# Scattering the gates of an expert lookup: a kernel whose one-hot matrices move from two engines to one

## The reference, cut to what matters

```python
def _peer(x, wq, k1, k2, u_tab, v_tab):
    ...
    sc, pos = lax.top_k(cand, PEER_TOPK)                      # 16 of the candidates, for each of 8 heads
    eidx = jnp.take_along_axis(cidx, pos, axis=-1).reshape(T, PEER_HK)     # 128 experts of 16384 a token
    gate = jax.nn.softmax(sc.astype(jnp.float32), axis=-1).astype(x.dtype).reshape(T, PEER_HK)
    ...
        act = jax.nn.gelu(jnp.einsum('td,tkd->tk', xb, ub), approximate=False)
        vb = jnp.take(v_tab, ib, axis=0)
        return jnp.einsum('tk,tkd->td', gb * act, vb)
```

## Time and profile before

| | |
|---|---|
| three executions | 3152.38, 3154.97, 3155.89 us; median 3154.97 |
| the profiled execution, first to last instruction | 3147.6 us |
| median less that span | 7.4 us |
| PE busy | 2982.5 us, 95% |
| DVE busy | 2251.5 us, 72% |
| ACT busy | 1839.0 us, 58% |
| POOL busy | 1117.7 us, 36% |
| mean granted TensorE clock | 0.974 of full speed |
| gelu of pair 17 to gelu of pair 57, first lookup | 1483.00 to 1767.08 us |
| the same, second lookup | 2468.20 to 2752.02 us |

### The profile page before, as it was taken

One profiled execution on the slowest core, in us unless ns is written; L12 is line 12 of the kernel. 1 busy time (PEld: TensorE's weight loads), 2 busy tenths in 40 slices (PEclk: granted clock), 3 DMA queues, 4 the chain that ended last, 5 costly groups with the idle time before them and its releaser, 6 DMA issues.

```text
span 3147.6 us, 48399 instructions
## 1 busy us (share of the span) xinstructions
PE 2982.5 (95%) x17718; PEld 2613.9 (83%) x17718; DVE 2251.5 (72%) x3884; ACT 1839.0 (58%) x2813; POOL 1117.7 (36%) x1033
## 2 busy tenths in 40 slices
PE   7889999897999979898999999998989999999998
PEld 7768888776888857798999988887789999988887
DVE  5459999345899976598565487776579765557777
ACT  4658888444788855455555555555554555555554
POOL 3420000432000005688767501014569767620100
PEclk9989999998999989999999999999999999999999
DMA  5359999532899953465665677775346655677776
GB/s 205 114 189 350 374 370 370 182 141 86 303 374 369 365 187 118 134 188 192 191 185 181 211 248 238 245 239 183 128 135 213 186 189 180 186 237 245 240 243 205
DMA packets 203995, 701.76 MB, mean 223 GB/s; under 512 B 23602, under 2 KB 24754, under 8 KB 203504
## 3 DMA queue, kind: packets, MB, share of 16 engines
q1 hardware_dynamic: 170640, 619.07, 58.1%
q10 hardware_dynamic: 21056, 40.07, 3.5%
q0 software_dynamic: 12064, 39.52, 3.2%
HBM read 659.77 MB, written 38.80 MB: 222 GB/s over the span
## 4 chain that ended last, share of the span: by engine, by line
PE 87%; DVE 6%; POOL 3%; ACT 2%; DMA 1%; issue 1%; ACTq 0%; DVEq 0%; SPq 0%; POOLq 0%
PE ps L592 85%; POOL splitb L533 3%; PE ps L603 2%; DVE hrow L105 1%; DVE arena L95 1%; DVE arena L105 1%; ACT splitb L506 1%; DMA rawb<-in_peer_u 1%; DVE arena L100 0%; DVE hL L95 0%; DMA hrow<-in_x_rows 0%; ACT hH L159 0%; DMA spill<-gb 0%; ACT arena L159 0%; DMA rawb<-in_s_out 0%
## 5 line engine op out<-in xcount | busy, mean ns | idle before, releaser
L506 ACT ACTIVATE splitb<-rawb 128x512 fp32r<-128x512 f32 (+1 forms) x1306 | 826.7, 639 | 851.8 <-PE ps L592 708.4
L533 POOL TENSOR_TENSOR splitb<-rawb,splitb 128x512 fp32r<-128x512 f32 x571 | 775.3, 1374 | 855.9 <-ACT splitb L506 848.7
L592 PE MATMUL ps<-hH,splitb 128*128 128x256 f32 x5248 | 987.8, 287 | 18.8 <-POOL splitb L533 16.4
L592 PEld LDWEIGHTS ps<-hH,splitb 128*128 128x128 f32 x5248 | 836.9, 194 | 26.1 <-issue 14.3
L533 DVE TENSOR_TENSOR splitb<-rawb,splitb 128x512 fp32r<-128x512 f32 (+1 forms) x735 | 524.7, 733 | 409.1 <-ACT splitb L506 407.0
L592 PE MATMUL ps<-splitb,hid 128*128 128x512 f32 x3444 | 788.8, 389 | 2.6 <-ACT hid L159 2.6
L592 PEld LDWEIGHTS ps<-splitb,hid 128*128 128x128 f32 x3444 | 646.1, 188 | 138.4 <-ACT hid L159 3.4
L592 PE MATMUL ps<-hL,splitb 128*128 128x256 f32 x2624 | 747.2, 285 | 0.0
L592 PEld LDWEIGHTS ps<-hL,splitb 128*128 128x128 f32 x2624 | 508.4, 194 | 0.9 <-issue 0.5
L592 PE MATMUL ps<-experts_r 128*128 128x512 f32 (+2 forms) x1364 | 338.3, 397 | 16.5 <-ACT experts_r L159 9.0
L592 PEld LDWEIGHTS ps<-experts_r 128*128 128x128 f32 (+1 forms) x1364 | 256.6, 194 | 72.5 <-ACT experts_r L159 7.5
(11 more groups left out here) (163 smaller groups left out, 3320.2 us busy)
## 6 DMA issues: line engine op xcount, KB each, us to landing
rawb<-in_peer_u SPq DMA_DIRECT2D x256, 512.0 KB, 3.7
rawb<-in_peer_v SPq DMA_DIRECT2D x256, 512.0 KB, 4.2
experts<-in_moe_gu SPq DMA_DIRECT2D x228, 512.0 KB, 5.5
experts<-in_moe_d SPq DMA_DIRECT2D x108, 512.0 KB, 5.3
rawb<-in_moe_gu SPq DMA_DIRECT2D x92, 512.0 KB, 5.5
spill<-gb ACTq DMA_DIRECT2D x128, 256.0 KB, 4.2
aux<-spill POOLq DMA_DIRECT2D x128, 256.0 KB, 4.4
rawb<-in_moe_d SPq DMA_DIRECT2D x52, 512.0 KB, 5.5
```

The lines of the kernel that those rows point to most:

```text
L506: self.eng.activation(S.split(m)[0], S.raw(n)[:, off:off + w], ACT.Copy).then_inc(S.hi.sem, S.hi.step(("half", m)))
L533: self.eng.tensor_tensor(l, raw, h.bitcast(F32), ALU.subtract).then_inc(self.low.sem, self.low.step(("half", m), *([("raw", n)] if last el ...
L592: return self.eng.matmul(o, w, x, start=start, stop=stop)
```

## The change

For a token there is now one fp32r matmul of 128 x 256 in place of an fp32 one of 128 x 128. Its moving operand holds the i1 one-hot twice, times the high part and times the low part of the gate (`low` is gate minus its fp32r rounding; `dve_low_gates` makes it once for all tokens). The high and the low page stand beside each other in PSUM: for two tokens (a `k`), one bank. ScalarE copies the low page to `Gt` (`act_high_sum`), VectorE then adds the high page from PSUM (`dve_sum`). VectorE makes all one-hots: for two tokens one TENSOR_TENSOR of 128 x 256 and two SCALAR_TENSOR_TENSORs of 128 x 256. GpSimd makes no one-hots and all low halves up to pair 57. There are three sets of one-hots instead of five, and four PSUM banks (`accs`) that the up phase did not use before. Tokens are scattered after each tile instead of after each pair.

```diff
-            put(dram["peer_u"][layer, i], lo="dve" if i // 2 >= SCATTER and i // 2 % 2 == 0 else "pool")
+            put(dram["peer_u"][layer, i], lo="dve" if i // 2 >= SCATTERED and i // 2 % 2 == 0 else "pool")
...
+def twos(tile):
+
+    first, last = (min(128, max(0, 64 * (i - 2 * SCATTER) // (SCATTERED - SCATTER))) for i in (tile, tile + 1))
+    return range(first, last)
...
         for p in range(64):
-            self.pe_pair(pe, p)
+            b = pe.open("p.u", n, p)
+            for j in range(2):
+                pe.proj(b[:, 256 * j:256 * j + 256], ("p.u", n, p))
+                for k in twos(2 * p + j):
+                    self.pe_scatter(pe, k)
...
+    def pe_scatter(self, pe, k):
+
+        S, n = self.S, self.layer
+        pe.wait_ge(S.vdone, "p.a", n, k)
+        if k >= 4:
+            pe.wait_ge(S.vdone, "p.Gt", n, k - 4)
+        for j in range(2):
+            ins = pe.mm(S.accs[k % 4][:, 256 * j:256 * j + 256], self.hot[k % 3][:, j, :],
+                        self.weight[k % 3][:, j, :, :].rearrange("p s n -> p (s n)"), True, True)
+        pe.out(ins, ("p.G", n, k))
...
+    def act_high_sum(self, act, k):
+
+        S, n = self.S, self.layer
+        b = S.accs[k % 4].rearrange("p (j s i) -> p j s i", j=2, s=2)
+        act.wait_ge(S.product, "p.G", n, k)
+        act.cp(self.Gt[:, 2 * k:2 * k + 2, :], b[:, :, 1, :], ("p.Gh", n, k))
...
         for p in range(64):
-            for t0 in groups(p):
-                self.dve_scatter(dve, t0)
+            if p == SCATTER:
+                self.dve_low_gates(dve)
+            for j in range(2):
+                for k in twos(2 * p + j):
+                    self.dve_hot(dve, k)
+                    if k >= 3:
+                        self.dve_sum(dve, k - 3)
+            if p == SCATTERED - 1:
+                for k in (125, 126, 127):
+                    self.dve_sum(dve, k)
...
+    def dve_hot(self, dve, k):
+
+        S, n = self.S, self.layer
+        iota, iT, m = S.C["iota"], self.iT, 2 * k
+        dve.wait_ge(S.vdone, "p.gl", n, m // 128)
+        if k >= 3:
+            dve.wait_ge(S.product, "p.G", n, k - 3)
+        dve.tt(self.hot[k % 3], bc(iota, 1, 2), bc(iT[:, 1, m:m + 2], 2, 128), ALU.is_equal, own=False)
+        for j in range(2):
+            low = S.aux_r[:, 512 + m + j:513 + m + j].bitcast(F32)
+            gates = bass.AP(low.tensor, low.offset, [list(low.ap[0]), [2304 - 512, 2], [0, 128]])
+            dve.stt(self.weight[k % 3][:, j, :, :], bc(iota, 1, 2), iT[:, 0, m + j:m + j + 1], gates, ALU.is_equal,
+                    ALU.mult, ("p.a", n, k), own=False)
+
+    def dve_sum(self, dve, k):
+
+        S, n = self.S, self.layer
+        b = S.accs[k % 4].rearrange("p (j s i) -> p j s i", j=2, s=2)
+        G = self.Gt[:, 2 * k:2 * k + 2, :]
+        dve.wait_ge(S.acted, "p.Gh", n, k)
+        dve.tt(G, b[:, :, 0, :], G, ALU.add, ("p.Gt", n, k), own=False)
...
-            for t0 in groups(p):
-                self.pool_scatter(pool, t0)
             pool.fed(2)
```

More of the change, by code:

```diff
@@ L292 @@
 ROUND = 8388608.0
-def groups(p):
-    first, last = (min(64, max(0, 64 * (i - SCATTER) // (SCATTERED - SCATTER))) for i in (p, p + 1))
-    return [4 * g for g in range(first, last)]
+def twos(tile):
+    first, last = (min(128, max(0, 64 * (i - 2 * SCATTER) // (SCATTERED - SCATTER))) for i in (tile, tile + 1))
+    return range(first, last)
 class Shared:
@@ L319, in __init__ @@
         self.cst = sb("cst", cw)
-        self.aux = sb("aux", max(places(w)[1] for w in (AB_AUX, C_AUX, S_AUX)))
+        width = max(places(w)[1] for w in (AB_AUX, C_AUX, S_AUX))
+        with nc.sbuf_tensor("aux", [128, width], F32) as aux:
+            self.aux = aux
+        self.aux_r = sb("aux_r", width, F32R)
         self.rt = sb("rt", 2 * 180)
@@ L2620, in __init__ @@
         self.Gt = S.arena[:, :].rearrange("p (t i) -> p t i", i=128)
-        self.AB = [x.rearrange("p (s j n) -> p s j n", s=2, j=2)
-                   for x in [S.aux[:, 768 + 512 * i:1280 + 512 * i] for i in range(3)] +
-                   [S.gb[:, 512 * i:512 * i + 512] for i in range(2)]]
+        room = [S.aux_r[:, 768 + 768 * i:1536 + 768 * i] for i in range(2)] + [S.hid[:, 0:768]]
+        self.hot = [x[:, 0:256].rearrange("p (j n) -> p j n", j=2) for x in room]
+        self.weight = [x[:, 256:768].rearrange("p (j s n) -> p j s n", j=2, s=2) for x in room]
+        self.high_gate = S.aux_r[:, 2304:2560]
         self.hb = [S.aux[:, 512 * i:512 * i + 512] for i in range(3)]
@@ L2734, in act_early @@
         ring = S.load(f"spill{n}_{i % 2}")
-        act.fed(2)
+        act.fed()
+        for k in twos(2 * i):
+            self.act_high_sum(act, k)
+        act.fed()
         act.wait_ge(S.product, "p.u", n, i)
@@ L2741, in act_early @@
         act.eng.dma_start(S.spill.ap()[n, i, :, :], r).then_inc(ring.sem, ring.step(("spill", i)))
+        for k in twos(2 * i + 1):
+            self.act_high_sum(act, k)
+    def act_high_sum(self, act, k):
[3 more added lines that the diff above has]
+        act.cp(self.Gt[:, 2 * k:2 * k + 2, :], b[:, :, 1, :], ("p.Gh", n, k))
     def act_choice(self, act, t):
@@ L2877, in dve_gates, with dve_low_gates @@
         dve.tt(g3, g3, bc(gs[:, 8:16], 2, 16), ALU.mult, ("p.sel", n, t))
-    def dve_scatter(self, dve, t0):
+    def dve_low_gates(self, dve):
         S, n = self.S, self.layer
[L2881 to L2893, removed]
+        for t in range(2):
+            g = self.iT[:, 2, 128 * t:128 * t + 128]
+            dve.wait_ge(S.acted, "p.iT", n, t)
+            dve.tt(S.aux_r[:, 512 + 128 * t:640 + 128 * t], g, self.high_gate[:, 128 * t:128 * t + 128].bitcast(F32),
+                   ALU.subtract, ("p.gl", n, t))
+    def dve_hot(self, dve, k):
[16 more added lines that the diff above has]
+        dve.tt(G, b[:, :, 0, :], G, ALU.add, ("p.Gt", n, k), own=False)
     def pool(self, pool):
@@ L2914, in pool_back @@
         else:
-            pool.wait_ge(S.acted, "p.G", n, 252)
+            pool.wait_ge(S.vdone, "p.Gt", n, 127)
         ring = S.load(f"back{n}_{i % 3}")
         pool.eng.dma_start(self.hb[i % 3], S.spill.ap()[n, i, :, :]).then_inc(ring.sem, ring.step(("back", i)))
[L2919 to L2928, removed]
 def build(nc, dram, out):
```

27 lines of the change are left out of this document (3 added, 24 removed).

## The result

The changed kernel takes 3269.11 us (median of four executions, 3264.90 to 3276.91) where the kernel before took 3153.68 in the same rounds: ratio 1.0368, 95% interval 1.0353 to 1.0384. It is 3.7% slower. The forecast was 3280 us, range 3200 to 3335. The profiled execution spans 3265.6 us, 118.0 more than before.

What follows compares the result with a forecast made beforehand. VectorE, waiting for GpSimd's low halves, was to replace TensorE as the bound of pairs 18 to 57: 3147.6 profiled + 121 + 6 for the ends = 3275, with 7.4 around the span 3282, taken as 3280 us; range 3200 to 3335.

Steps and rivals of the forecast that it cites:

- TensorE's gain: Pairs 18 to 57: TensorE needs 6.53 us a pair, 0.66 less; 52 us over both lookups if the cover holds.
- The mechanism: Pairs 18 to 57: VectorE's two-SBUF-input one-hots and GpSimd's low halves exclude each other, VectorE becomes the bound; 80%.
- The sizes: VectorE's pair: 4.83 us work plus 4.40 lost to low halves less 0.54 hidden, 8.69 us; +121 us for both lookups.
- The ends: Start at pair 18 costs 1 us, last tokens at pair 57 cost 2 us; 6 us for two lookups.
- The clock: TensorE, 75% active in the stage, was expected to stay at 2.4 GHz, granted clock 1.00; at 1.2 GHz 3627 us.
- the cover holds: Rival for pairs 18 to 57: TensorE stays the bound at 6.53 us a pair, total 3109 us; 6%.
- The rule on the two engines: Skill's full blocking between VectorE and GpSimd: whole 1.3 us lost per low half, 9.5 us a pair, about 3345 us.

Runs made afterwards that it cites:

- iota_psum: Changed kernel with the one-hots' table of column numbers read from a PSUM bank, token-result banks three instead of four; 3118.45 us, ratio 0.9872.
- pool_write: Changed kernel, but GpSimd fills the low halves of pairs 18 to 57 with zeros by MEMSET, left out of the result; 3116.34 us, ratio 0.9874.
- after_late: Changed kernel with the scatter starting at pair 19 in place of 18, column numbers still in SBUF; 3272.88 us, ratio 1.0372.
- fill: Changed kernel with four more 256-column matmuls on TensorE ahead of the wait for each two tokens' one-hots; 3286.45 us, ratio 1.0422.
- iota_best: Changed kernel with column numbers in PSUM, three result banks, scatter from pair 19 and pair 58's low halves on GpSimd; 3108.08 us, ratio 0.9851.
- ring3: Changed kernel with three PSUM banks in place of four for token results, column numbers still in SBUF; 3274.60 us, ratio 1.0377.
- pool_read: Changed kernel, but GpSimd writes low halves of pairs 18 to 57 as zero times raw, one SBUF input, left out of the result; 3126.05 us, ratio 0.9898.

## Why the prediction was right, step by step

*TensorE's gain.* Right: 6.53 us for a pair was said; the runs without exclusion have 6.54 and 6.55, and the fast pairs of the changed kernel 6.46. Of the 52 us for both lookups, less 6 at the ends, the fastest run has 45 (3153.23 less 3108.08).

*The mechanism.* Right, and shown from both sides (iota_psum, pool_write). VectorE was named as the bound and is busy for 96%; the additions stay at 0.41; the long group is one per low half: for pairs 19 to 57 the trace has 146 one-hot operations over 0.7 us beside 152 low halves. One detail was off: the long SCALAR_TENSOR_TENSORs lie at 1.48 to 1.58 us, as said, but half of the long TENSOR_TENSORs are under 1.2.

*The sizes.* For two tokens 1.51 us was said and 1.46 measured. The loss for each low half, net of what an addition hides: said (4.40 - 0.54) / 4 = 0.965, measured in the stage (172 x 0.842 + 84 x 0.846 - 256 x 0.473 + 86 x 0.765 + 42 x 0.728 - 128 x 0.41) / 157 = 0.88. Pairs 18 to 57 then make 128 x 1.46 + 157 x 0.88 = 325 us of 339, and VectorE's own idle time is 12 of the rest, for which I had only the 1 us at the start. Two errors of opposite sign: a pair takes 8.37 us (said 8.69), some 22 us less over both lookups (8.44 in the second), but the first interval is 7.8 us longer than before where I had 2.5, some 11 us more over both. That the total came within 11 us of the forecast is in part the luck of this offset. The 7.4 us around the span were no constant either: the profiled execution took 3267.36 us for its span of 3265.6, and the median less the span is now 3.5.

*The ends.* At pair 57: 57 to 60 takes 2.2 and 0.9 us more than before, said 2. At pair 18 my 1 us was wrong in kind: after_late shows that TensorE's wait is not a term of the sum under a bound on VectorE; the 3 us until VectorE's first one-hot are.

*The clock.* Wrong. I expected 1.00 from a row with 78% of activity. TensorE is at 1.2 GHz in thirteen stretches of the first stage, 51 of 339 us in all. The row had waits of up to 1.6 us; here they are longer. An even loss had been assumed, 1.1 us for each tile; in truth TensorE runs at full pace for a pair or more and then waits for up to 2.9 us at once (5.65 at the start), and the stretches begin at such waits. With VectorE as the bound it cost little: no gain that fill would show, and in the first stage at most the 8 us in which VectorE waits for TensorE. TensorE is busy for 85%, not 75%: 6.53 of 8.37 us would be 78%, and its matmuls are slower in the stretches. The rule of the Trainium skill (TensorE: Matmul & The Clock Gate, "HAM oscillation — how this bites in real kernels") tells of matmul loops that fall back to the lower clock in every gap; I had weighed it against the row and put it aside. The trace agrees in kind, with 13 stretches at 0.50 in the first stage, but not every gap had one.

*The rival "the cover holds".* It had 6% and did not come. Its time, 3109, is near that of the kernels without the exclusion: 3118 (iota_psum) and 3116 (pool_write), and 3108 only with the later start and pair 58's low halves moved (iota_best).

*The rule on the two engines.* The Trainium skill (SBUF — State Buffer, "Who interferes with whom") has the later instruction blocked until the other has finished. For a two-input instruction on GpSimd the trace comes near it: of a low half's 1.26 to 1.60 us, a long SCALAR_TENSOR_TENSOR loses 1.04 on average and a long TENSOR_TENSOR 0.73. That a GpSimd instruction which only writes holds nothing up agrees with pool_write. For one that reads a single operand, a block for the whole instruction does not hold: at most 0.43 of 1.51 us.

## What to carry to other kernels

Before moving work between VectorE and GpSimd, look in the trace for the maximum beside the median of each operation's duration, and for who runs when it is reached; adding up busy shares would have called this change safe (VectorE 74%, GpSimd 80% of the pair). If both must run, give VectorE's operation one operand in PSUM or GpSimd's none to read: here one table of 128 columns in PSUM turned 3.7% slower into 1.3% faster. And when one engine bounds a stage, waits of the others in it, their clock and their start add to its time only where the bounding engine comes to wait for them in turn: here 8 of 339 us.

## What the runs showed of the hardware that I had not expected

- A single wait of TensorE of 2.7 us, in a stage in which it is busy for 85%, was followed by 3.4 to 6.8 us at 1.2 GHz (granted clock 0.50).
- The second lookup of ring3 had only 3.4 us of that in pairs 19 to 57 and was 9.5 us shorter than the first (323.1 and 332.6 us). Its trace shows another rhythm: after one wait of 3.0 us TensorE waits 43 times, for 1.35 us at most, and no slow stretch follows any of them; in the first lookup eleven waits are of 2.7 to 3.1 us. VectorE, the bound, stands idle for 4.4 us in place of 19.8, most of it for TensorE, and is busy for 318.7 in place of 312.8. So the rhythm of the waits can cost the bounding engine time; why the same program falls into one or the other is not shown.
- A TENSOR_SCALAR of 128 x 512 with one input takes GpSimd 1.51 us beside a busy VectorE, longer than the 1.32 to 1.40 us of a two-input low half, and yet takes less than a third as much from VectorE (0.26 against 0.88 to 0.99 us; VectorE idles more in pool_read, but the longest hold-up differs as well, 0.43 against 1.11 us).
- With one operand in PSUM there is no loss left on either side, where I had expected a little: in the same 255.5 us GpSimd's 152 low halves are busy for 195.96 us, 1.29 each, their median in the kernel before, and VectorE's one-hot operations take 0.42 and 0.475.
